# Forgetting attention: scores from stacked halves, one value sum per pair of heads, keys projected first, and an out projection that begins in the last pair

## The reference, cut to what matters

```
def odd_mixer(h, w_in, b_f, w_out):                    # 16 heads of 64, 512 tokens
    q, k, v, f = split_cols(h @ w_in, ODD_SPLITS)      # three times 1024 columns, and 16
    log_f = jax.nn.log_sigmoid((f + b_f).astype(jnp.float32))
    o = forgetting_attention(q, k, v, log_f)
    return o @ w_out

# in forgetting_attention, for each block of 128 queries:
    s = einsum('bqhd,bshd->bhqs', qb, k) * scale
    s = s + (cq[..., :, None] - cum[..., None, :])     # cum: running sum of log_f
    p = masked_softmax(s, kpos[None, :] <= tpos[:, None])
    out = einsum('bhqs,bshd->bqhd', p, v)
```

## Time and profile before

| | |
|---|---|
| median of 3 runs | 3185.72 us (3179.16 to 3191.79) |
| the profiled execution | 3189.51 us, its span 3188.1 us |
| mean granted TensorE clock | 0.975 of full |
| TensorE busy | 3039.2 us, 95% of the span |
| VectorE, ScalarE, GpSimd busy | 2220.6, 1295.4, 801.0 us |
| `fox`, first scores to first out projection matmul | 782.0 to 990.2 us |

### The profile page before, as it was taken

How to read it: one execution, slowest core, us unless ns; L and a number is a source line. 1 busy time by engine, 2 the same in 40 slices (tenths; PEclk the granted TensorE clock), 3 DMA queues, 4 the chain that set the end, 5 groups by cost and what they waited for, 6 DMA issues and landing times. The chain is left out here.

```text
span 3188.1 us, 43523 instructions
## 1 busy us (share of the span) xinstructions
PE 3039.2 (95%) x16376; PEld 2616.7 (82%) x16376; DVE 2220.6 (70%) x4318; ACT 1295.4 (41%) x2272; POOL 801.0 (25%) x696
## 2 busy tenths in 40 slices
PE   7999999999999999988989989999989999999998
PEld 5666788887666888866767868999989999999997
DVE  4766486774555876843443458978788888888886
ACT  3656432233444322333432233349843333343333
POOL 1000100001001200033000023678734435334431
PEclk9999899999999999988999989999999999999998
DMA  4001244333221544321122223565699999999993
GB/s 145 28 28 53 69 159 146 130 106 115 77 67 62 176 134 144 103 70 55 44 70 92 93 80 98 179 202 209 235 341 330 322 355 326 331 327 324 329 327 112
DMA packets 189711, 525.36 MB, mean 165 GB/s; under 512 B 15792, under 2 KB 80176, under 8 KB 187200
## 3 DMA queue, kind: packets, MB, share of 16 engines
q1 hardware_dynamic: 130432, 308.84, 28.7%
q0 software_dynamic: 45104, 164.68, 14.7%
q10 hardware_dynamic: 13968, 49.06, 4.0%
HBM read 484.22 MB, written 38.31 MB: 164 GB/s over the span
## 5 line engine op out<-in xcount | busy, mean ns | idle before, releaser
L239 PE MATMUL bank<-h_hi,w_hi 128*128 128x512 f32 (+1 forms) x2528 | 966.5, 382 | 49.4 <-ACT w_hi L207 16.3
L239 PE MATMUL bank<-h_lo,w_hi 128*128 128x512 f32 (+1 forms) x2528 | 948.7, 375 | 0.0
L213 DVE TENSOR_TENSOR w_lo<-w_raw,w_hi 128x1024 fp32r<-128x1024 f32 (+1 forms) x452 | 580.6, 1285 | 297.0 <-ACT w_hi L207 294.4
L207 ACT ACTIVATE w_hi<-w_raw 128x1024 fp32r<-128x1024 f32 (+1 forms) x508 | 545.2, 1074 | 508.6 <-PE bank L239 488.9
L239 PEld LDWEIGHTS bank<-h_hi,w_hi 128*128 128x128 f32 x2528 | 483.4, 191 | 140.4 <-issue 37.8
L239 PE MATMUL bank<-h_hi,w_lo 128*128 128x512 f32 (+1 forms) x2528 | 596.2, 372 | 0.1
L239 PEld LDWEIGHTS bank<-h_lo,w_hi 128*128 128x128 f32 x2528 | 484.4, 192 | 64.0 <-issue 8.7
L239 PEld LDWEIGHTS bank<-h_hi,w_lo 128*128 128x128 f32 x2528 | 459.4, 189 | 68.6 <-issue 12.3
L239 PE MATMUL bank<-e_hi,w_hi 128*128 128x384 f32 x1024 | 345.5, 337 | 11.1 <-DVE e_lo L2357 11.1
L239 PE MATMUL bank<-e_lo,w_hi 128*128 128x384 f32 x1024 | 345.0, 337 | 0.0
L2265 POOL DMA_INDIRECT own_row<-in_u_rows,own_e x128 | 165.6, 1294 | 273.1 <-DVE sums L2394 214.9
(11 more groups left out here) (406 smaller groups left out, 4343.1 us busy)
## 6 DMA issues: line engine op xcount, KB each, us to landing
w_raw<-in_w SPq DMA_DIRECT2D x476, 512.0 KB, 3.8
ada_w<-in_ada_w POOLq DMA_DIRECT2D x48, 512.0 KB, 3.6
expert_weights<-G ACTq DMA_DIRECT2D x12, 2048.0 KB, 7.1
Gin<-expert_weights SPq DMA_DIRECT2D x32, 768.0 KB, 9.6
w_raw<-in_w SPq DMA_DIRECT2D x32, 704.0 KB, 4.1
hidden_ahead<-u_stage ACTq DMA_DIRECT2D x56, 192.0 KB, 3.9
ahead<-hidden_ahead SPq DMA_DIRECT2D x28, 384.0 KB, 6.7
fx_crow<-fox_cum POOLq DMA_DIRECT2D x8, 512.0 KB, 5.7
```

The costliest lines, as they stand in the source:

```text
L207: sc.activation(w_hi[s][:, 0:n], w_raw[raw_slot[u]][:, 0:n], ACT.Copy).then_inc(*w_hi_made.next(u))
L213: ve.tensor_tensor(w_lo[s][:, 0:n], w_raw[raw_slot[u]][:, 0:n], w_hi[s][:, 0:n], ALU.subtract).then_inc(*w_lo_made.next(u))
L239: m = te.matmul(out, wt, moving, start=(not low and k == 0 and moving is hi), stop=(low and k == len(blocks) - 1))
```

## The change

It touches `fox`, its helpers, the two units of the out projection that stand first, and the order of the weight tiles in memory (key, query, values instead of query, key, values).

- **Stacked scores.** The query of a head is stored as its high part on the head's own 64 partitions and its low part on the other 64. The key's high part is stored twice, on both halves, and so is its low part. Two fp32r matmuls over all 128 partitions then give the full product, in place of one fp32 matmul over 64. ScalarE gets 6 copies of 64x512 for each pair, VectorE 6 subtractions of 64x512.
- **Sums per pair.** The transposed probabilities of all four steps are kept in one buffer per head, and the value sums are made once per pair, in step 0 of the next: for key block j one matmul of (4-j)*128 columns for each head.
- **Order and spread.** The key unit stands first. Each of the three places of a step runs 6 projection matmuls. The value transposes stand in step 0 of the pair that uses them, behind the transposes of probabilities, not at the end of the pair before.
- **Out projection.** Its first unit runs over seven of its eight blocks and its second as far as 15 of its 24 matmuls (12 pieces of 3 matmuls in all) inside the last pair; the last block of each waits for the eighth pair. ScalarE leaves out `split_hi` behind the first of the units (`ahead`), since that part has been made in the pair.
- The buffers of bias rows (`fx_crow`) go from four to two.

The diff, cut to its core:

```diff
+    def late_unit(u, out, blocks, ready):
+        s, last, step = u % 2, len(blocks) - 1, 0
+        te.wait_ge(*w_hi_made.at(u))
+        te.wait_ge(*bank_of.at(u - 2))
+        for k, low in [(k, low) for low in (False, True) for k in range(last)] + [(last, False), (last, True)]:
+            w, hi, lo = blocks[k]
+            if low and k == 0:
+                te.wait_ge(*w_lo_made.at(u))
+            if not low:
+                te.wait_ge(*ready(w))
+            for moving in (hi,) if low else (hi, lo):
+                m = te.matmul(out, (w_lo if low else w_hi)[s][:, w * P:(w + 1) * P], moving, start=(step == 0), stop=(step == 3 * last + 2))
+                step += 1
+                if step == 3 * len(blocks):
+                    m.then_inc(*w_used.next(u))
...
-    def out_scalar(name, U, then=None, gain=None):
+    def out_scalar(name, U, then=None, gain=None, ahead=0):
         for n, u in enumerate(U):
-            split_hi(u + 1)
+            if n >= ahead - 1:
+                split_hi(u + 1)
...
+    def ahead_units(U, hi, lo, ready, order):
+        blocks = [(k, hi[:, k, :], lo[:, k, :]) for k in order]
+        return [late_unit(u, lin[u % 2][:, :], blocks, ready) for u in U[:2]]
...
+                if n < len(begun):
+                    run(begun[n])
+                else:
+                    run(unit(u, [(lin[u % 2][:, :], blocks)], ready if n == 0 else None))
...
+    def query_hi(B, name, p):
+        sc.wait_ge(*dve.at(name, "q", p))
+        for hh in range(2):
+            rows = head_rows(hh)
+            sc.activation(q[p % 2][rows, hh, :], qf[rows, :], ACT.Copy).then_inc(*act.next(name, "q hi", p))
...
+    def query_lo(B, name, p):
+        ve.wait_ge(*act.at(name, "q hi", p))
+        for hh in range(2):
+            rows = head_rows(hh)
+            ve.tensor_tensor(q[p % 2][beside(hh), hh, :], qf[rows, :], q[p % 2][rows, hh, :], ALU.subtract).then_inc(*dve.next(name, "q lo", p))
...
+    def key_hi(B, name, p):
+        sc.wait_ge(*dve.at(name, "k", p))
+        for hh in range(2):
+            rows = head_rows(hh)
+            for to in (rows, beside(hh)):
+                sc.activation(k_hi[p % 2][to, hh, :], kf[rows, :], ACT.Copy).then_inc(*act.next(name, "k hi", p))
...
+    def key_lo(B, name, p):
+        ve.wait_ge(*act.at(name, "k hi", p))
+        for hh in range(2):
+            rows = head_rows(hh)
+            for to in (rows, beside(hh)):
+                ve.tensor_tensor(k_lo[p % 2][to, hh, :], kf[rows, :], k_hi[p % 2][rows, hh, :], ALU.subtract).then_inc(*dve.next(name, "k lo", p))
...
+    def stacked_scores(out, q, k_hi, k_lo, hh, tile, keys):
+        te.matmul(out, q[:, hh, tile], k_hi[:, hh, keys], start=True, stop=False)
+        return te.matmul(out, q[:, hh, tile], k_lo[:, hh, keys], start=False, stop=True)
...
+    def stacked_scalar(U, B, name, p):
+        yield
+        split_hi(U[0] + 1)
+        yield
+        yield
+        split_hi(U[1] + 1)
+        key_hi(B, name, p)
+        yield
+        yield
+        split_hi(U[2] + 1)
+        query_hi(B, name, p)
+        yield
+    def stacked_vector(U, B, name, p, gain=None, flip=False):
+        yield
+        split_lo(U[0] + 1)
+        yield
+        ve.wait_ge(*w_used.at(U[0]))
+        scaled(kf[:, ::-1] if flip else kf[:, :], lin[U[0] % 2][:, :]).then_inc(*dve.next(name, "k", p))
+        bank_of.taken(U[0], dve)
+        yield
+        split_lo(U[1] + 1)
+        yield
+        key_lo(B, name, p)
+        yield
+        ve.wait_ge(*w_used.at(U[1]))
+        if gain is None:
+            scaled(qf[:, :], lin[U[1] % 2][:, :]).then_inc(*dve.next(name, "q", p))
+        else:
+            ve.scalar_tensor_tensor(qf[:, :], lin[U[1] % 2][:, :], gain, ny[:, :], ALU.mult, ALU.mult).then_inc(*dve.next(name, "q", p))
+        bank_of.taken(U[1], dve)
+        yield
+        query_lo(B, name, p)
+        yield
+        split_lo(U[2] + 1)
+        ve.wait_ge(*w_used.at(U[2]))
+        scaled(vT[:, ::-1] if flip else vT[:, :], lin[U[2] % 2][:, :]).then_inc(*dve.next(name, "v", p))
+    def turn_values(U, B, name, p):
+        te.wait_ge(*dve.at(name, "v", p))
+        turn(B[6], lin[U[2] % 2], TT).then_inc(*pe.next(name, "v turned", p))
+    def take_values(U, B, name, p):
+        sc.wait_ge(*pe.at(name, "v turned", p))
+        turned(B[5][p % 2][:, :, :], lin[U[2] % 2], TT).then_inc(*act.next(name, "ready", p))
+        bank_of.taken(U[2], act)
...
-        PT = [[sb(st, f"fx_pt{hh}{b}", [P, TT, P]) for b in range(2)] for hh in range(2)]
+        PT = [sb(st, f"fx_pt{hh}", [P, 3 * TT + 1, P]) for hh in range(2)]
...
+        crow = [sb(st, f"fx_crow{s}", [P, 2, T]) for s in range(2)]
...
+        def pair_units(p):
+            for u in U[p]:
+                yield from h_unit(u)
+        def sums_of(p):
+            for hh in range(2):
+                te.wait_ge(*act.at("fx moved", hh, 4 * p + TT - 1))
+            te.wait_ge(*act.at("fx", "ready", p))
+            if p >= 2:
+                te.wait_ge(*dve.at("fx out", p - 2))
+            for j in range(TT):
+                for hh in range(2):
+                    rows = head_rows(hh)
+                    t = te.matmul(o_banks[p % 2][rows, j * P:T], v[p % 2][:, j, rows], PT[hh][:, 4 * j:3 * j + TT, :], start=(j == 0), stop=(j == TT - 1))
+                    if j == TT - 1:
+                        t.then_inc(*pe.next("fx sums", hh, p))
...
-                    more = pair_tensor(U[p + 1], buffers, "fx", p + 1) if p < 7 else iter(())
+                    more = pair_units(p + 1) if p < 7 else itertools.chain(itertools.islice(begun[0], 7), itertools.islice(begun[1], 5)) if p == 7 else iter(())
+                    a, b = (2, 1 << 30) if p < 7 else (1, 1)
                 for hh in range(2):
-                    rows = head_rows(hh)
                     if m < steps:
                         if i == 0:
-                            te.wait_ge(*act.at("fx", "ready", p))
-                            te.wait_ge(*dve.at("fx", "k", p))
+                            te.wait_ge(*dve.at("fx", "q lo", p))
+                            te.wait_ge(*dve.at("fx", "k lo", p))
                         if m:
                             te.wait_ge(*dve.at("fx least", hh, m - 1))
-                        te.matmul(s_bank[hh][:, 0:kw], q[p % 2][rows, i * P:(i + 1) * P], k[p % 2][rows, 0:kw], start=True, stop=True).then_inc(*pe.next("fx scores", hh, m))
-                run(more, 2)
+                        stacked_scores(s_bank[hh][:, 0:kw], q[p % 2], k_hi[p % 2], k_lo[p % 2], hh, slice(i * P, (i + 1) * P),
+                                       slice(0, kw)).then_inc(*pe.next("fx scores", hh, m))
+                run(more, a)
                 for hh in range(2):
                     if m:
                         p2, i2 = divmod(m - 1, TT)
                         was = Pm[hh][(m - 1) % 2]
                         te.wait_ge(*dve.at("fx probs", hh, m - 1))
+                        if m >= 2:
+                            te.wait_ge(*act.at("fx moved", hh, m - 2))
                         for j in range(i2 + 1):
                             t = te.transpose(t_bank[hh][:, j * P:(j + 1) * P], was[:, j * P:(j + 1) * P], ident[:, :])
                         t.then_inc(*pe.next("fx turned", hh, m - 1))
-                run(more, 2)
-                if m:
-                    for hh in range(2):
-                        te.wait_ge(*act.at("fx moved", hh, m - 1))
-                    if i2 == 0 and p2 >= 2:
-                        te.wait_ge(*dve.at("fx out", p2 - 2))
-                    for j in range(i2 + 1):
-                        for hh in range(2):
-                            rows = head_rows(hh)
-                            t = te.matmul(o_banks[p2 % 2][rows, i2 * P:(i2 + 1) * P], v[p2 % 2][:, j, rows], PT[hh][(m - 1) % 2][:, j, :],
-                                          start=(j == 0), stop=(j == i2))
-                            if j == i2:
-                                t.then_inc(*pe.next("fx sums", hh, m - 1))
-                run(more, 3 if i < TT - 1 else 1 << 30)
+                if i == 0 and m < steps:
+                    turn_values(U[p], B, "fx", p)
+                run(more, a)
+                if m and i == 0:
+                    sums_of(p - 1)
+                run(more, a if i < TT - 1 else b)
...
+                if p == 7 and i == 1:
+                    split_hi(V[1])
                 if m:
                     p2, i2 = divmod(m - 1, TT)
+                    if i2 == 0 and p2:
+                        for hh in range(2):
+                            sc.wait_ge(*pe.at("fx sums", hh, p2 - 1))
...
+                if p == 7 and i == 2:
+                    split_lo(V[1])
...
-                if p >= 4:
-                    gp.wait_ge(*dve.at("fx least", 1, 4 * (p - 3) - 1))
-                gp.dma_start(crow[p % 4][:, :, :], cum_dram[2 * p:2 * p + 2, :].unsqueeze(0).to_broadcast([P, 2, T])).then_inc(*crow_in[p % 4].next(p))
+                if p >= 2:
```

(3 more changed lines are left out.)

88 lines of the change are left out of this document (53 added, 35 removed).

## The result

The changed kernel takes 3156.8 us (median of four runs, 3154.6 to 3159.3), the kernel before 3183.2 (3179.2 to 3191.8): ratio 0.9915, interval [0.9903, 0.9927]. So 26.5 us are won where 19.2 were forecast. It is faster by more than 0.5%, and inside the range of 3155 to 3182.

The account below looks back on a forecast made before the run. TensorE, busy 95% of the span, was taken as the bound. Start 1.0, pair 0 3.8, pairs 1 to 6 15.0, last pair and out projection -0.6 sum to 19.2 us: median 3166.5 (chance 0.55), range 3155 to 3182.

Parts of the forecast that it names:

- The pair: Each of pairs 1 to 6: 2.5 us less, so 25.0 us instead of 27.48, 15.0 us over the six.
- scores: Score matmuls of both heads in a pair: 2.60 us in single-pass stacked form instead of 3.02, 0.42 won.
- edges: Projection matmuls next to scores or sums cost about 0.1 us extra; 11 such places go, 0.9 us won per pair.
- sums: Value sums of a pair: one group of 2.3 us instead of several totalling 2.76, 0.46 won.
- value wait: TensorE's wait for VectorE's value copy before the value transposes: 0.45 us per pair instead of 1.03, 0.58 won.
- hand count of VectorE: VectorE's queue timed from a pair's first scores: low part to 15.4 us, value copy done at 28.4.
- the early out projection pays and the value wait goes: Rival, chance 0.15: 36 early matmuls fill 4.2 us idle in the last pair, the 0.45 wait vanishes; 3159 us.
- Pair 0: First pair: 23.2 us instead of 26.95, 3.8 won, with 1.5 us kept for TensorE's lower clock level.
- Start: Before the first scores: they need not wait for the values, so they come 1.0 us earlier.
- last pair with out projection: From the last pair's first scores to the end: 62.0 us instead of 61.4, 0.6 lost despite 36 matmuls moved early.
- VectorE as the bound: Rival, chance 0.05: subtractions crossing partitions cost 1.23 us each, pairs take 28.2, total 3195; decides from about 1.08 each.
- halves of wide sums: Rival, chance 0.07: the two column halves don't overlap in wide sums, 2.2 us more in each of 8 pairs; 3184.

## Why the prediction was right, and where not

*The bound* was right: TensorE's matmuls set the pair, and taking work, edges and waits from them shortens it. The total, 19.2 forecast for 26.5, was too small, and the terms below say where; the measured 3156.8 lies only 1.8 us inside the lower end of the range, which was set by the case of full gain.

*The pair, 2.5 forecast, 3.2 measured, 4.3 us over six.* By the distances of a full pair: scores 0.49 (forecast 0.42), edges 1.07 (0.9), sums 0.47 (0.46), value transposes 0.24 (0.17), the other transposes 0.1 dearer, and the value wait 1.03 (0.58). The last is the mis-sized term: the wait is gone whole. The hand count of VectorE has the value copy done 28.4 us after the pair's first scores; it is done after 26.8. Of these 1.6 us 1.1 stand already at its first figure, the weight's low part at 15.4, which ends at 14.3 and whose working the prediction doesn't show. The other 0.5 come behind that, where the count added durations, 1.23 and 0.69, for starts that are 1.14 and 0.60 apart. I had used distances for TensorE and not for VectorE, though the earlier trace rows show 0.61 between two starts there; the held subtractions (0.72) took little of that back. The step from the count to the wait has a slip as well: 28.4 is 3.4 behind a zero of 25.0, not 3.1, so by its own figures the wait was 0.8. The rival that the early out projection pays and the value wait goes had the wait right.

*Pair 0, 3.8 forecast, 5.9 measured.* Of the 2.1, some 0.6 are what every pair won beyond the forecast, and 1.5 the stretch at the lower clock level, which I took over as if it were a cost of the place. It was not: the kernel before had a granted clock of 0.58 there behind waits of 0.79 and 0.69, the changed one has 1.00 behind a single wait of 1.13. The rows of before could not tell which of the two levels would come.

*Start* 1.0, and *last pair with out projection* 61.2 for 62.0: resumption after 23.4 for 24.3, wait for the high part 0.9 for 1.2 (the figures given for it, 2.92 less 2.1, make 0.8). Each is right within 1 us, but the sentence drawn from them, "so the early start gives back what it takes", is wrong. I compared two kernels that differ in two things there. The wide sums cost the last pair 5.9 us when nothing stands beside them (22.25 for 16.31), of which 2.4 go with the lower clock, and the early start brings 6.1 back in all; with sums in every step it would have brought 2.0, with the plain scores as well 0.95.

*The rivals.* VectorE as the bound did not come: 0.72 for a subtraction, against a limit of 1.08. But it was nearer than its chance says: four more subtractions take the pair to 27.10, and the old place of the value transposes would have given back 23.4 of the 26.4 us. The halves of wide sums overlap. The case in which the early out projection pays and the value wait goes, forecast at 3159, is the nearest to the measured 3156.8, and it had 0.15; the forecast with 0.55 lay 9.7 us off. Of the 9.7, 7.2 are gain that the sum did not have; the other 2.5 lie in the kernel before, whose median was 3183.2 in these runs and 3185.7 in those that the forecast started from. What stays open is which waits of 2.4 us bring the lower clock and which don't.

## What to carry to other kernels

Add up distances between starts on every engine of a hand count, not only on the one that bounds: here the value copy had 0.15 us to spare, and durations alone put it 0.5 too late. A saving per iteration that gathers work into one piece (here, the sums once per pair) must be charged at the last iteration, where nothing stands beside it, and the filling that is put there is worth what the gathering cost: judge them together or leave one out at a time. And a stretch at the lower clock level does not belong to its place in the kernel: here it went when the waits in front of it changed. Where waits change, forecast with both clocks, since equal waits of 2.4 us had either behind them.

## What the runs showed of the hardware

- Single-pass matmuls cost by their columns down to 256: 0.234 us from start to start at 512, 0.17 at 384, 0.12 at 256; at 128 it is 0.11, hardly less. Next to the stacked scores, of full height like the projection, no edge of 0.1 us shows; with plain scores the edges are 0.76 us of a pair more.
- VectorE operations of 512 columns over 64 partitions take as long as over 128 (0.68 to 0.69 us each); from start to start it is 0.72 with the halves alternating and 0.60 behind a copy over all 128.
- The last sums took 4.4 us instead of 2.4 behind a wait of 2.00 in a stretch in which TensorE had been busy for half of the time (granted clock 0.52). Two waits of 2.37 and 2.38 in full pairs had a clock of 0.67 and of 1.00 behind them.
